# Adding the last expert's rows to the accumulator's tiles: a scatter through memory against matmuls with a matrix of zeros and ones

## The reference

```
for e in range(16):
    ye = (silu(hf @ w_gate[e]) * (hf @ w_up[e])) @ w_down[e]
    out = out + combine[:, e:e + 1] * ye
x = x1 + gt2 * out
y = x * rsqrt(mean(x * x) + 1e-6) * g_final
```

## Time and profile before

| | us |
|---|---|
| median of 3 runs | 964.49 (962.38 to 967.12) |
| the profiled execution's own time | 965.28 |
| its span in the profile | 963.5 |
| busy in the span: TensorE | 855.8 |
| VectorE | 708.6 |
| ScalarE | 414.9 |
| GpSimd | 302.8 |

### The profile page before, as it was taken

One profiled execution on the slowest core, in us unless ns is written; L12 is line 12 of the kernel. 1 busy time (PEld: TensorE's weight loads), 2 busy tenths in 40 slices (PEclk: granted clock), 3 DMA queues, 4 the chain that ended last, 5 costly groups with the idle time before them and its releaser, 6 DMA issues. The chain is left out here.

```text
span 963.5 us, 12777 instructions
## 1 busy us (share of the span) xinstructions
PE 855.8 (89%) x5225; PEld 714.8 (74%) x5225; DVE 708.6 (74%) x939; ACT 414.9 (43%) x379; POOL 302.8 (31%) x176
## 2 busy tenths in 40 slices
PE   3799999998989999989999994799999999999930
PEld 3688888898988798889994543578887877777720
DVE  2437999999895896992024466789989988897818
ACT  5242322223246323241201213467777777776703
POOL 5226546635530110143311140113312543250010
PEclk9899999999999999999999996799999999999965
DMA  9966777422120140342446104689999999999733
GB/s 322 291 207 230 251 261 245 151 91 88 44 88 1 45 132 1 102 133 88 159 148 247 45 31 193 204 293 349 366 372 332 342 342 361 353 361 326 281 84 118
DMA packets 76680, 194.55 MB, mean 202 GB/s; under 512 B 8075, under 2 KB 49163, under 8 KB 66237
## 3 DMA queue, kind: packets, MB, share of 16 engines
q1 hardware_dynamic: 71245, 182.19, 53.3%
q0 software_dynamic: 5232, 11.16, 4.4%
q10 hardware_dynamic: 144, 0.38, 0.1%
HBM read 185.41 MB, written 17.00 MB: 210 GB/s over the span
## 5 line engine op out<-in xcount | busy, mean ns | idle before, releaser
L743 POOL TENSOR_TENSOR w_lo<-ring_a,w_hi 128x2048 fp32r<-128x2048 f32 x28 | 131.7, 4704 | 240.8 <-ACT w_hi L926 240.8
L1787 DVE TENSOR_TENSOR slot_c<-ring_a,slot_c 128x2048 fp32r<-128x2048 f32 x72 | 164.0, 2289 | 22.9 <-ACT slot_c L1065 22.7
L1269 PE MATMUL ps<-hm_hi,w_hi 128*128 128x272 f32 x720 | 152.5, 293 | 6.9 <-POOL w_lo L743 2.6
L1065 ACT ACTIVATE slot_c<-ring_a 128x2048 fp32r<-128x2048 f32 x72 | 137.2, 1916 | 44.0 <-DMA ring_a<-in_w_gate 27.3
L1269 PE MATMUL ps<-hm_hi,w_lo 128*128 128x272 f32 x720 | 149.4, 290 | 0.0
L1269 PE MATMUL ps<-hm_lo,w_hi 128*128 128x272 f32 x720 | 148.9, 289 | 0.0
L1619 DVE SCALAR_TENSOR_TENSOR ps<-region_b,rt,ps 128x512 f32<-128x512 f32 x208 | 137.6, 746 | 0.0
L1269 PEld LDWEIGHTS ps<-hm_hi,w_hi 128*128 128x128 f32 x720 | 113.4, 190 | 22.1 <-issue 17.8
L1431 PE MATMUL ps<-slot_c,xgt_hi 128*128 128x512 f32 x384 | 126.3, 399 | 2.4 <-DVE slot_c L1787 1.2
L1269 PEld LDWEIGHTS ps<-hm_lo,w_hi 128*128 128x128 f32 x720 | 113.6, 190 | 0.0
L1269 PEld LDWEIGHTS ps<-hm_hi,w_lo 128*128 128x128 f32 x720 | 113.4, 190 | 0.0
(11 more groups left out here) (313 smaller groups left out, 1409.3 us busy)
## 6 DMA issues: line engine op xcount, KB each, us to landing
ring_a<-in_w_gate SPq DMA_DIRECT2D x32, 1024.0 KB, 8.1
ring_a<-in_w_up SPq DMA_DIRECT2D x32, 1024.0 KB, 8.7
ring_a<-in_w_down SPq DMA_DIRECT2D x32, 1024.0 KB, 7.3
ring_a<-in_w_in SPq DMA_DIRECT2D x24, 1024.0 KB, 6.9
region_c<-in_w_ada SPq DMA_DIRECT2D x20, 1024.0 KB, 5.6
ring_a<-in_w_conf_o SPq DMA_DIRECT2D x4, 1024.0 KB, 6.7
ring_a<-in_w_lru_o SPq DMA_DIRECT2D x4, 1024.0 KB, 5.2
region_d<-in_w_ada SPq DMA_DIRECT2D x3, 1024.0 KB, 13.3
```

The source lines that it names most:

```text
L743: g.tensor_tensor(w_lo[:, q % 2], raw[split_at[q] % 2], w_hi[:, q % 2].bitcast(F32), ALU.subtract)\
L1065: s_.activation(hi_slot(n), raw_slot(n), ACT.Copy).then_inc(unit_hi, 1)
L1269: ins = mm(ps[:, bank(n) + h, 0:HALF], w[:, q % 2, k, m * P:(m + 1) * P], x[:, k, h * HALF:(h + 1) * HALF], start=(k == 0 and w is w_hi an ...
L1787: v.tensor_tensor(lo_slot(n), raw_slot(n), hi_slot(n).bitcast(F32), ALU.subtract).then_inc(unit_lo, 1)
```

## The change

Experts 0 to 14 keep their way. For expert 15, ScalarE writes the weighted rows' high part to `row_hi`, VectorE the low part to `row_lo`. VectorE builds `hot`, 128 x 544, ahead of expert 13's step (they count from 0): a one where the column's token is the slot's token. For each tile TensorE adds into two PSUM banks: the tile of `ya` times a unit matrix (`sums_before`), and `hot`'s columns of that tile by `row_hi` and by `row_lo` (`last_expert`). VectorE's multiplication by `gt2` reads the banks in place of `ya`. Tiles 0 and 2 end in another way: ScalarE scales the tile (`scaled`) and GpSimd multiplies it by `g_final`. The output tiles have five places in place of two. SyncE waits for the last low part in place of the last use of a unit before it reads the flag.

```diff
+BY_POOL = (0, 2)
...
             for n in range(RAWS, len(units)):
                 load_unit(n)
-            sp.wait_ge(unit_used, len(units))
+            sp.wait_ge(unit_lo, len(units))
             sp.wait_ge(ov_ok, 1)
...
             for t in range(NT):
-                sp.wait_ge(fin_ok, t + 1)
+                if t in BY_POOL:
+                    sp.wait_ge(fin_pool, BY_POOL.index(t) + 1)
+                else:
+                    sp.wait_ge(fin_ok, t + 1 - sum(i < t for i in BY_POOL))
...
             pool.wait_ge(lg_ps, NT)
             g.tensor_copy(tok6[:, :, :, 0:2], tokid[:, :, :].unsqueeze(2).to_broadcast([P, NT, NE, 2])).then_inc(tok_ok, 1)
-            for e in range(NE + XGS):
+            ch.link(g.iota(tok_tmp, pattern=[[1, T]], base=0, channel_multiplier=0))
+            g.tensor_copy(iota_tok, tok_tmp).then_inc(tok_ok, 1)
+            for e in range(NE - 1 + XGS):
...
             pool.wait_ge(y_store[0], 16 * (NE // 2))
-            pool.wait_ge(y_store[1], 16 * (NE // 2))
+            pool.wait_ge(y_store[1], 16 * (NE // 2 - 1))
...
+            for i, t in enumerate(BY_POOL):
+                pool.wait_ge(scaled_ok, i + 1)
+                g.tensor_tensor(yo[:, t, :], scaled, gfin_bc, ALU.mult).then_inc(fin_pool, 1)
...
-            y_rows(NE - 1)
+            act.wait_ge(unit_used, len(units))
+            act.wait_ge(w_slot_ok, NE)
+            s_.activation(row_hi.rearrange("p (h n) -> p h n", h=2), ps[:, 5:7, :], ACT.Copy,
+                          scale=w_slot[:, NE - 1:NE]).then_inc(y_act, 1)
...
                 s_.activation(junk[0:n, :], x1[0:n, t, :], ACT.Square, accum_out=ssq[0:n, t:t + 1]).then_inc(fin_act, 1)
+                if t - 1 in BY_POOL:
+                    i = BY_POOL.index(t - 1)
+                    act.wait_ge(rs_ok, i + 1)
+                    if i:
+                        act.wait_ge(fin_pool, i)
+                    s_.activation(scaled, x1[:, t - 1, :], ACT.Copy, scale=rstd[:, t - 1:t]).then_inc(scaled_ok, 1)
                 act.wait_ge(rms_ask, NT + t + 2)
...
+            def sums_before(t):
+
+                n, b = TILES[t], 2 * (t % 2)
+                pe.wait_ge(rows_in[t], 32)
+                if t >= 2:
+                    pe.wait_ge(fin_dve, t - 1)
+                for h in range(2):
+                    mm(ps[0:n, b + h, :], ident[0:n, 0:n], ya[0:n, t, h * 512:(h + 1) * 512], start=True, stop=False)
+
+            def last_expert(t):
+
+                n, b = TILES[t], 2 * (t % 2)
+                pe.wait_ge(hot_ok, 1)
+                pe.wait_ge(y_act, NE)
+                for h in range(2):
+                    mm(ps[0:n, b + h, :], hot[:, t * P:t * P + n], row_hi[:, h * 512:(h + 1) * 512], start=False, stop=False)
+                pe.wait_ge(row_lo_ok, 1)
+                for h in range(2):
+                    ins = mm(ps[0:n, b + h, :], hot[:, t * P:t * P + n], row_lo[:, h * 512:(h + 1) * 512],
+                             start=False, stop=True)
+                ins.then_inc(sum_ps, 1)
+
+            sums_before(0)
+            sums_before(1)
+            for t in range(NT):
+                last_expert(t)
+                if t + 2 < NT:
+                    sums_before(t + 2)
...
             for e in range(6, NE):
+                if e == NE - AHEAD:
+
+                    dve.wait_ge(tok_ok, 2)
+                    v.tensor_scalar(hot[:, :], iota_tok, idx_t[:, 0:1], None, ALU.is_equal).then_inc(hot_ok, 1)
                 step(e)
+            dve.wait_ge(y_act, NE)
+            v.scalar_tensor_tensor(row_lo.rearrange("p (h n) -> p h n", h=2), ps[:, 5:7, :], w_slot[:, NE - 1:NE],
+                                   row_hi.bitcast(F32).rearrange("p (h n) -> p h n", h=2), ALU.mult, ALU.subtract)\
+             .then_inc(row_lo_ok, 1)
...
                 if t < NT:
                     n = TILES[t]
                     y1, xr = ya[0:n, t, :], x1[0:n, t, :]
-                    dve.wait_ge(rows_in[t], 32)
+                    dve.wait_ge(sum_ps, t + 1)
...
                 if t < NT:
-                    ch.do(v.tensor_tensor(y1, y1, gt2_bc[0:n, t // 4, :], ALU.mult))
+                    ch.do(v.tensor_tensor(y1.rearrange("p (h n) -> p h n", h=2), ps[0:n, 2 * (t % 2):2 * (t % 2) + 2, :],
+                                          gt2_bc[0:n, t // 4, :].rearrange("p (h n) -> p h n", h=2), ALU.mult))
...
-                    ch.link(v.scalar_tensor_tensor(r_, q_, 1.5, r_, ALU.add, ALU.mult))
-                    if t >= 3:
-                        dve.wait_ge(y_out[(t - 1) % 2], 16 * ((t - 1) // 2))
-                    v.scalar_tensor_tensor(yo[0:n_, (t - 1) % 2, :], x1[0:n_, t - 1, :], rstd[0:n_, t - 1:t],
-                                           gfin_bc[0:n_, :], ALU.mult, ALU.mult).then_inc(fin_ok, 1)
+                    ins = v.scalar_tensor_tensor(r_, q_, 1.5, r_, ALU.add, ALU.mult)
+                    if t - 1 in BY_POOL:
+                        ins.then_inc(rs_ok, 1)
+                    else:
+                        ch.link(ins)
+                        v.scalar_tensor_tensor(yo[0:n_, t - 1, :], x1[0:n_, t - 1, :], rstd[0:n_, t - 1:t],
+                                               gfin_bc[0:n_, :], ALU.mult, ALU.mult).then_inc(fin_ok, 1)
```

More of the change, by code:

```diff
@@ L100, in build @@
             xgt_lo = under.enter_context(nc.sbuf_tensor("xgt_lo", [P, KC, P], F32R))
+            hot = under.enter_context(nc.sbuf_tensor("hot", [P, T], F32R))
         region_b = sb("region_b", [P, 12288])
@@ L182, in build @@
         ya = carve(ring_a, 0, (NT, D))
-        yo = carve(region_c, 0, (2, D))
+        yo = carve(region_c, 7168, (NT, D))
         junk = carve(region_c, 2 * D, (D,))
+        scaled = carve(region_c, 3 * D, (D,))
+        row_hi, row_lo = slot_c[:, 1, 0, 0:D], slot_c[:, 1, 1, 0:D]
+        iota_tok = region_b[:, 640:640 + T]
+        tok_tmp = region_b[:, 9472 + D:9472 + D + T].bitcast(I32)
         unit_raw = [carve(ring_a, s * UNIT, (UNIT,)) for s in range(RAWS)]
@@ L379, in build @@
         ov_done = sem("ov_done")
+        hot_ok = sem("hot_ok")
+        row_lo_ok = sem("row_lo_ok")
+        sum_ps = sem("sum_ps")
+        rs_ok = sem("rs_ok")
+        scaled_ok = sem("scaled_ok")
+        fin_pool = sem("fin_pool")
         fin_dve = sem("fin_dve")
@@ L662, in _ @@
             with sp.If(n_over > 0):
+                sp.wait_ge(unit_used, len(units))
                 with sp.Fori(0, n_over) as k:
@@ L678, in _ @@
             for t in range(NT):
-                sp.wait_ge(fin_ok, t + 1)
+                if t in BY_POOL:
+                    sp.wait_ge(fin_pool, BY_POOL.index(t) + 1)
+                else:
+                    sp.wait_ge(fin_ok, t + 1 - sum(i < t for i in BY_POOL))
                 dst = a["yp"][0, t * P:(t + 1) * P, :] if t < NT - 1 else a["ys"].rearrange("s t d -> (s t) d")
-                sp.dma_start(dst, yo[0:TILES[t], t % 2, :]).then_inc(y_out[t % 2], 16)
+                sp.dma_start(dst, yo[0:TILES[t], t, :]).then_inc(y_out[t % 2], 16)
             sp.wait_ge(y_out[0], 16 * 3)
```

## The result

The change made the kernel **slower: 971.44 us against 963.37 us** (medians of 8 runs each), a ratio of 1.0079 with a 95% interval of 1.0058 to 1.0101. The forecast was 967.0 with a range up to 970.3 and "no change" as the likeliest.

A forecast was written before the change was run, and what follows sets the result against it. VectorE was taken to bound the tail, which starts after a chain of waits for memory. The terms -4.7 + 2.1 + 2.1 + 1.3 + 1.7 = +2.5 us, on the median of 964.49, gave 967.0; range 961.0 to 970.3.

The forecast's parts named there:

- Part 2: Tail's start: TensorE's first group enters the path; VectorE begins 4.7 us sooner at the lower clock level, 6.6 at the upper.
- Part 1: Tail's start: GpSimd waits for expert 14's add alone, so tile 0 lands at 927.3; reads hide the last rows' split.
- Part 3: Tail passes: VectorE waits for TensorE's two groups; 2.1 us lost in each of three passes, 0.5 at the upper level.
- Part 4: GpSimd's two tiles: tile 2's multiplication holds VectorE's addition in the pass of tile 4, 1.7 us lost.
- The clock: TensorE's level in the tail: lower for three groups, half and half for the last; all lower +3.3, all upper -2.2.
- Rival (a): TensorE stays at the upper clock level in the tail: -2.2 us, 962.3; chance 0.18.
- tile 0's lock: GpSimd's multiplication of tile 0 holds VectorE's addition in tile 2's pass; at the upper level 4.8 us becomes 6.0.
- Rival (c): GpSimd's multiplication of tile 2 takes 4.82 us, not 2.35: 2.5 more, +5.8 at the lower level, 970.3; slower's chance 0.20.

The follow-up runs named there:

- e3_sums_twice: The changed kernel with the two `sums_before` matmuls of each tile done twice, the second over the first's result; one execution 975.24 us, tail 52.2 us.
- e5_keep_busy: The changed kernel with extra matmuls into an unused bank in TensorE's pauses; ratio 1.0016 to the kernel before, median 963.42 against 962.60 us.
- e2_no_pool: The changed kernel with no tile ending on GpSimd, all five on VectorE; ratio 1.0059 to the kernel before, tail 40.9 us.
- e1_order: The changed kernel with the last expert's matmuls of tile 1 queued ahead of tile 2's earlier sums, and so on; ratio 0.9974, median 958.75 against 961.62 us.

## Why the prediction was wrong

**The step that failed is a price in Part 2.** The forecast had the direction (+2.5), not the size. "`sums_before` is two float32 matmuls of 512 columns, 7.11 / 16 = 0.444 each": the row's x16 counts instructions, and the code behind that row has 8 matmuls in it (one tile, one half, 8 blocks of the sum). A float32 matmul shows as two instructions and costs 0.89 at the upper level (0.92 in e3_sums_twice, 1.95 for two in e5_keep_busy), and about 1.8 at the lower (3.59 for two in e2_no_pool). The Trainium skill (FP8 and Floating Point Precision, "TensorE Precision Notes") has a true float32 matmul go through the array four times; the trace agrees, with 0.89 against 0.235 for a float32r one of that width, a factor of 3.8.

With that term doubled and the rest left, the prediction's own steps give, at the upper level, a first group of 3.6 + 0.9 + 0.2, so VectorE 5.3 sooner, hand-overs of 3.1 and passes of 5.7: -5.3 + 3 x 1.4 + 1.7 = +0.6. In e5_keep_busy, all at the upper level, the tail has +0.2. At the lower level VectorE comes 1.2 sooner, with hand-overs of 5.5 and passes of 8.1: -1.2 + 3 x 3.8 + 1.7 = +11.9. The measured +7.0 lies between, since the groups ran partly at either level. So the range would have reached well past 970.3, with slower as the likeliest.

A second term was off, the other way. With the prediction's choice of levels (the lower for three groups, half and half for the last) the right price gives -1.2 + 3.8 + 3.8 + 2.6 + 1.7 = +10.7, 3.7 more than measured. That the forecast missed by no more than it did is luck: one error hid a part of the other.

Point by point:

- *Part 1* held: GpSimd went on 4.73 after the issue's end (4.65 forecast), its branch took 1.15, the first read 3.73 (3.69). The split and the branch were hidden.
- *Part 3*, the mechanism, held: `last_expert` of the next tile behind `sums_before` of the one after it, VectorE waiting at the head of its pass, and the scalings taken off VectorE paying nothing. e1_order shows what the order is worth, with the clock that came with it: 37.9 in place of 46.0. Hand-overs of 4.4, 4.6 and 5.2 took the place of the forecast 3.8.
- *Part 4* held: 5.70 for the pass of tile 4 against a forecast 6.0, and 4.3 without GpSimd. Tile 0's multiplication was over before the addition of tile 2 was due, as forecast for long hand-overs.
- *The clock* was the unknown the prediction named, and it differs between executions. e5_keep_busy shows its size: with the pauses filled the change costs 0.16% (-0.11 to 0.44) in place of 0.79%. The Trainium skill (TensorE: Matmul & The Clock Gate, "What's actually happening") has the throttled state as the default, which activity releases. Taken as strictly as in the sum, that does not fit this tail: after pauses of 2.7 and 2.8 us the second and the third group began at 1.00 and fell within.
- *Rival (a)*, all groups at the upper level, was to give -2.2; e5_keep_busy has that level and +0.2, by the price of above. The range's lower end takes 1.3 off (a) for tile 0's lock, where the sum's own terms have 1.2; nothing hangs on it.
- *Rival (c)*, the slower one, did not happen: GpSimd took 2.34 and 2.37 us, not 4.82. The slow side came from TensorE.

What stays open is which groups fall to the lower level and why it differs between executions, and why executions of e5_keep_busy reach 968.80; only one of them was profiled.

## What to carry to other kernels

Count instructions of a row against the operations in the code before a duration is divided by the row's count; a float32 matmul is two of them. When a step is put between two halves of another engine's pass, look at what is queued behind its waits: here one changed order of TensorE's queue was worth 8 us of the tail, and enough banks to remove the waits, with all tiles ending on VectorE, made the same idea 0.65% faster than before. Work moved to an engine beside which the bottleneck's own operations take longer can cost more than it takes off: here 1.4 us for each tile on GpSimd.

## What the runs showed of the hardware that was not expected

- TensorE's granted clock fell within groups of some 4.3 us that stood between pauses of 2.7 to 2.8 us, and two matmuls of one shape took 1.95 us (e2_no_pool, the sums of tile 2, all at 1.00) or 3.52 (those of tile 3, mostly at 0.50). Filling the pauses with matmuls nobody reads held it at 1.00 in the profile and brought the time down from 0.79% above the kernel before to 0.16% above.
- Doubling the work of a group could leave the clock up: eight instructions in 3.67 us in e3_sums_twice, against four in 3.52 in e2_no_pool, after the same pause of 2.80 us.
